# State-space groups: the second turn of xs moved into the middle of the gate chunk, its copy moved ahead of that gate

## The reference

```
def mamba2_bidir_mixer(x, w_in, conv_w, conv_b, dt_bias, a_log, d_skip, norm_w, w_out):
    zxbcdt = x @ w_in
    z, xbc, dt = jnp.split(zxbcdt, [SSM_D_INNER, SSM_D_INNER + SSM_CONV_DIM], axis=-1)
    xbc = jax.nn.silu(depthwise_conv_centred(xbc, conv_w, conv_b))
    xs, bm, cm = jnp.split(xbc, [...], axis=-1)
    dt = jax.nn.softplus((dt + dt_bias).astype(jnp.float32))
    y_f = ssd_chunked(xs, dt_f, a_neg[0], bm, cm)
    y_b = flip(ssd_chunked(flip(xs), flip(dt_b), a_neg[1], flip(bm), flip(cm)))
    y = (y_f + y_b).astype(x.dtype) + xs * d_skip[:, None]
    y = y.reshape(bsz, t, SSM_D_INNER) * jax.nn.silu(z)
    yg = yg * lax.rsqrt(jnp.mean(jnp.square(yg), -1, keepdims=True) + RMS_EPS)
    ...
    return y @ w_out
```

## Time and profile before

| | us |
|---|---|
| median of 3 runs | 1288.05 |
| lowest and highest | 1287.56, 1288.16 |
| the profiled execution's own time | 1287.21 |
| its span, first to last instruction | 1285.4 |
| TensorE busy in the span | 1254.6 |
| VectorE, ScalarE, GpSimd busy | 894.6, 711.4, 155.2 |
| mean granted TensorE clock | 0.995 of full |

### The profile page before, as it was taken

One profiled execution on the slowest core, in us unless ns is written; L12 is line 12 of the kernel. 1 busy time (PEld: TensorE's weight loads), 2 busy tenths in 40 slices (PEclk: granted clock), 3 DMA queues, 4 the chain that ended last, 5 costly groups with the idle time before them and its releaser, 6 DMA issues.

```text
span 1285.4 us, 19450 instructions
## 1 busy us (share of the span) xinstructions
PE 1254.6 (98%) x7940; PEld 1121.1 (87%) x7940; DVE 894.6 (70%) x1148; ACT 711.4 (55%) x909; POOL 155.2 (12%) x171
## 2 busy tenths in 40 slices
PE   8999999999799999999999999999999999999997
PEld 7889888889689888889888888889999989988886
DVE  6866656566866755568777665678899886866666
ACT  5445554455665555444764444447997873544442
POOL 0000000005604000010010000020325432100000
PEclk9999999999899999999999999999999999999999
DMA  8676665645059666666147555545544435555551
GB/s 281 201 227 178 209 196 179 200 152 191 34 147 213 204 191 196 197 164 215 66 135 255 199 185 184 187 144 161 157 153 122 153 99 193 201 196 196 196 190 41
DMA packets 214888, 224.52 MB, mean 175 GB/s; under 512 B 7312, under 2 KB 192016, under 8 KB 214672
## 3 DMA queue, kind: packets, MB, share of 16 engines
q1 hardware_dynamic: 211472, 213.41, 52.1%
q10 hardware_dynamic: 2304, 7.77, 1.8%
q0 software_dynamic: 1024, 2.10, 1.0%
HBM read 222.20 MB, written 1.05 MB: 174 GB/s over the span
## 4 chain that ended last, share of the span: by engine, by line
PE 84%; DVE 9%; ACT 3%; issue 2%; POOL 1%; DMA 1%; SPq 0%; DVEq 0%; ACTq 0%
PE ps L521 21%; PE ps L748 18%; PE ps L512 12%; PE ps L532 7%; PE ps L542 5%; PE ps L710 5%; PE ps L1040 3%; PE ps L504 3%; DVE wlo L1653 2%; PE ps L493 2%; PE ps L495 2%; PE ps L494 2%; DVE ssm_taps L2107 1%; ACT whi L1155 1%; PE ps L1021 1%
## 5 line engine op out<-in xcount | busy, mean ns | idle before, releaser
L1653 DVE TENSOR_TENSOR wlo<-raw,whi 128x2048 fp32r<-128x2048 f32 x199 | 456.5, 2300 | 127.0 <-ACT whi L1155 126.4
L1155 ACT ACTIVATE whi<-raw 128x2048 fp32r<-128x2048 f32 x202 | 385.3, 1910 | 87.9 <-PE ps L748 29.8
L521 PE MATMUL ps<-act,whi 128*128 128x512 f32 x1200 | 285.3, 390 | 0.4 <-DVE sum_sb L1796 0.4
L521 PEld LDWEIGHTS ps<-act,whi 128*128 128x128 f32 x1200 | 223.2, 188 | 45.7 <-DVE sum_sb L1796 0.7
L512 PEld LDWEIGHTS ps<-act,wlo 128*128 128x128 f32 x1416 | 180.8, 191 | 6.8 <-DVE wlo L1653 1.0
L512 PE MATMUL ps<-act,wlo 128*128 128x256 f32 x1416 | 183.9, 283 | 0.5 <-DVE wlo L1653 0.5
L1212 ACT ACTIVATE low_sb<-ps 128x512 f32<-128x512 f32 x88 | 52.4, 596 | 200.0 <-PE ps L512 199.9
L532 PE MATMUL ps<-whi,act 128*128 128x256 f32 x736 | 133.1, 285 | 1.1 <-DVE act L1734 1.1
L532 PEld LDWEIGHTS ps<-whi,act 128*128 128x128 f32 x736 | 113.5, 192 | 2.7 <-DVE act L1734 1.3
L1796 DVE TENSOR_TENSOR sum_sb<-ps,low_sb 128x512 f32<-128x512 f32 x88 | 60.5, 688 | 76.4 <-ACT low_sb L1212 76.3
L748 PE MATMUL ps<-whi,hidhi 128*128 128x512 f32 x336 | 104.2, 391 | 0.2 <-DVE sum_sb L1796 0.2
(11 more groups left out here) (238 smaller groups left out, 1848.4 us busy)
## 6 DMA issues: line engine op xcount, KB each, us to landing
raw<-in_mlp_w SPq DMA_DIRECT2D x128, 512.0 KB, 4.5
raw<-in_ffn_w_gate_up SPq DMA_DIRECT2D x88, 512.0 KB, 5.2
raw<-in_ssm_w_in SPq DMA_DIRECT2D x50, 512.0 KB, 4.8
raw<-in_ffn_w_down SPq DMA_DIRECT2D x44, 512.0 KB, 4.9
raw<-in_conv_w_in SPq DMA_DIRECT2D x24, 512.0 KB, 4.9
raw<-in_attn_w_in SPq DMA_DIRECT2D x18, 512.0 KB, 4.9
raw<-in_ssm_w_out SPq DMA_DIRECT2D x16, 512.0 KB, 4.5
raw<-in_attn_w_qkv SPq DMA_DIRECT2D x12, 512.0 KB, 4.4
```

Source lines behind the costliest of these rows:

```text
L521: e.matmul(bank2(b + f), hi[:, k, f * P:(f + 1) * P], act[:, :, k, :], start=k == 0, stop=False, skip_group_check=True)
L1155: e.activation(whi[s][:, :], raw[s][:, :], ACT.Copy).then_inc(*rounded.up(c))
L1653: e.tensor_tensor(wlo[s][:, :], raw[s][:, :], f32(whi[s][:, :]), ALU.subtract).then_inc(*split_by_vector.up(c))
```

## The change

On TensorE the turn of tile 1 of xs leaves its place behind step 5 (and, in groups 1 to 3, behind that step's outputs) and is issued inside step 5's chunk, between the 24 products of tile 0 and the 24 of tile 1. On ScalarE `copy_xs(G, 1)` moves from the head of the next group (in the last group, from behind the loop) to the place right ahead of `z_gate(2G + 1)`. Nothing is added or removed.

```diff
@@ pe_program, ssm @@
                         elif c is not None:
-                            token_chunk(c)
+                            token_chunk(c, None, [lambda: turn_xs(G, 1)] if k == 5 else ())
                             free[c % SLOTS] = z_gated(2 * G + k // 3)
...
                         if G == 0 and k == 5:
                             turn_parts()
-                        if k >= 4:
-                            turn_xs(G, k - 4)
+                        if k == 4:
+                            turn_xs(G, 0)
@@ act_program, ssm @@
                 for G in range(4):
                     n0 = 4 * (G - 1)
 
-                    if G:
-                        copy_xs(G - 1, 1)
                     if G == 1:
                         copy_gram(0)
...
                     conv_silu(4 * G + 3, G, 3)
+                    copy_xs(G, 1)
                     z_gate(2 * G + 1)
-                copy_xs(3, 1)
```

## The result

The changed kernel takes 1289.91 us (median of 20 runs, 1288.66 to 1293.95), the kernel before 1287.71 (20 runs beside it). The ratio is 1.0018, with a 95% interval of 1.0012 to 1.0024: 2.3 us slower, 1.5 to 3.1. The profiled execution has a span of 1288.0 us against 1285.4. Forecast were 1289.5 for the median, 1288.7 for the profiled execution, which took 1289.84, and a difference within 0.2%.

What follows compares the result with a forecast made beforehand. TensorE, busy 1254.6 of 1285.4 us, was taken as the bound. Group 0's 1.43 plus 0.10 for groups 1 to 3 gave 1.5 us, on 1288.05 a median of 1289.5; 8-in-10 range 1287.6 to 1290.9.

Steps and rivals of the forecast that it cites:

- Group 0: TensorE, chunk 5: the turn waits 0.96 us for ScalarE's bank read, plus 0.47 for transposes and refill; 1.43 later.
- It lasts: The 1.34 us wait ahead of item 1's outputs moves along with TensorE, so the 1.43 is carried through whole.
- rival 1: The delay is swallowed by the wait at 921.46; only about 0.2 us stays, 1288.2; chance 16%.
- Groups 1 to 3: TensorE: the moved turn doesn't wait; 0.05 us each in groups 1 and 2, 0 in group 3; 0.1 together.
- rival 2: The turn waits in all four groups, up to 0.96 us each, 1292.4; chance 11% with its lesser form.
- its lesser form: The same 1.4 us with a knock-on wait of about 1.3 in groups 0 and 1, 1290.8; within rival 2's 11%.
- ScalarE: Copy of xs and gate change places, 0.48 us apart, the next rounding keeping its time; worth 0.
- Rival 3: The copy ahead of the gate takes 0.48 us off each group's way to the next rounding, 1286.1; chance 4%.
- Group 3's wait for exponent rows shrinks by about 0.5: TensorE's 1.64 us wait in group 3 is shortened by the 0.47 added before it; no change in time.
- The clock: TensorE stays at full clock; a fall behind the moved turn, 8 us over four groups, 1297.5, had chance 2%.
- The rule weighed in the prediction: Transposes don't count as busy for the clock gate, which speaks against putting them with a wait into a chunk.
- the 1.5 of the mechanism: Sum over the groups, 1.43 in group 0 plus 0.10 in groups 1 to 3: 1.5 us slower; chance 67%.

Runs made afterwards that it cites:

- read_first: Changed kernel, but in group 0 ScalarE reads chunk 4's product out of its bank ahead of the rounding before it; ratio 1.0011 to the kernel before.
- before_again: The kernel before, unaltered, profiled once more; not timed against itself; its stretches sum to 196.59 us, as in the first profile.
- g0_only: Kernel before with the turn moved into the gate chunk in group 0 alone and the copy ahead of the gate in all groups; ratio 1.0012.
- g3_old: Kernel before with the turn moved in groups 0 to 2, left in its old place in group 3; ratio 1.0007.
- copy_first_old: Kernel before, but in group 0 ScalarE copies xs(0, 0) ahead of the exponent parts; ratio 0.9995.
- kept_busy: Changed kernel with seven unread 512-column matmuls in TensorE's wait for group 3's exponent rows, the gram-copy wait moved ahead of them; ratio 1.0006 to the kernel before.
- best_busy: Kernel best with six unread 512-column matmuls in front of the first product of y; median 1285.75 us, ratio 0.9985 to the kernel before.
- g3_only: Kernel before with the turn moved in group 3 alone and the copy ahead of the gate in all groups; ratio 1.0003.
- best: copy_first_old with, in group 3, VectorE making the exponent rows ahead of item 10's outputs; ratio 0.9990 to the kernel before.
- after_again: The changed kernel, unaltered, timed and profiled a second time; ratio 1.0013 to the kernel before.
- g0_old: Kernel before with the turn moved in groups 1 to 3 alone and the copy ahead of the gate in all groups; ratio 1.0004.
- copy_first_new: Changed kernel, but in group 0 ScalarE copies xs(0, 0) ahead of the exponent parts; ratio 1.0016 to the kernel before.

## Why the prediction was right, and where it was not

**Group 0.** The forecast was 0.96 of wait and 0.47 for transposes and refill, 1.43 in all. Measured were 1.45, and in read_first the two parts apart, 1.02 and 0.44. The grown wait (1.18, forecast about 1.2) shows that the old place gave nothing back. This is the one step that decides the sign.

**It lasts.** The wait in front of item 1 stayed (1.37), so rival 1 falls: "to item 1" is 22.98 or 22.99 in every kernel but the four that copy xs(0, 0) first.

**Groups 1 to 3.** The forecast was 0.1, measured was 0.06. There was no wait in front of the turn in any of them, so rival 2 falls with its lesser form.

**ScalarE.** The pair stands 0.47 apart in the other order in group 1, and the rounding behind it moved with TensorE (the first row is the kernel before's rounding, the others are the changed kernel's):

```profile
945.92 1.91 ACT L1155 ACTIVATE whi<-raw 128x2048 fp32r<-128x2048 f32 x1
...
945.95 0.57 ACT L1479 ACTIVATE xs<-ps 128x512 f32<-128x512 f32 x1
946.43 0.59 ACT L1401 ACTIVATE z<-ps 128x512 f32<-128x512 f32 x1
946.90 1.91 ACT L1155 ACTIVATE whi<-raw 128x2048 fp32r<-128x2048 f32 x1
```

The rounding starts 0.98 later by the span's time, which is the 1.45 less the 0.46 of the earlier start. Rival 3 falls.

**A sign that failed.** "Group 3's wait for exponent rows shrinks by about 0.5": it is 1.66 against 1.64. The 0.47 added ahead of the wait had been counted, the 0.36 to 0.44 taken away ahead of the same wait had not. It changed no sum.

**The clock.** This is the term that was missing. The prediction read the clock as 1.00 in the stretches that it had, took that as evidence that the mixture at the end of group 3 is safe, and gave a fall 2%, at a price of 8 us and in the wrong place, behind the turn in the chunk. The pace that it took for the lower level was right (0.205 a product, measured 0.21). The fall came at the end of group 3, in six of six profiles with the turn gone from there and the waits left as they were, and in none of the five with turn and waits as before (before, before_again, g0_only, g3_old, copy_first_old). It cost 1.0 to 2.4 us in them. Two interventions with matmuls in the idle time (kept_busy, best_busy) took it away, and this much of the cause is shown: the fall needs TensorE's idle time. That the missing transposes bring it is not shown. The profiles make it look like a rule. The timed executions say that it is at most a matter of how often, with 61% low against 41%. In g3_only, which has nothing but this difference and the swap of copy and gate, 8 of 11 are low against 12 of 27 of the kernel before beside it, too few to tell. So chance from one execution to the next stands as a rival that one profile of a kernel can't exclude.

The rule weighed in the prediction, of the Trainium skill ("TensorE: Matmul & The Clock Gate", Part 4, PE-mode transpose), says that transposes don't count as busy in the same way as other matmuls. By it, taking four away should leave the clock alone. The profiles of before and g3_only, whose other stretches are equal, speak against this, and the mean clocks of their timed executions, 0.9932 and 0.9934, don't. The runs settle it neither way.

**Why the number came out near.** Forecast were 1.5, measured 2.3 (1.5 to 3.1). The profiled execution has 1.45 + 0.06 + 1.12, and it took 1289.84, 1.1 more than the 1288.7 forecast for it. That the median of 1289.91 is only 0.4 over its forecast is in part luck: the forecast had added 0.84 for the distance between median and profiled execution, and in the changed kernel that distance was 0.07. How much of the median's rise is the fall is not settled. In g3_only it is 0.4 us in time against 2.3 in its profile. Among executions at 0.994 or above the changed kernel (14, both series) has a median of 1289.35 and the kernel before (61) one of 1287.58, 1.8 apart, nearer to the 1.5 of the mechanism. Open also is what decides between fall and full clock in an execution: the wait ahead of the decays is 1.64 in both before and g3_only, and what differs is the four transposes ahead of it.

## What to carry to other kernels

Before a step is moved forward on the engine that is the bound, find the instruction that releases it, and compare that one's end with the new place in each round of the loop, the first above all: here the other rounds had 2.4 us and more to spare by the forecast's rows and waited nowhere, and the first was 0.96 short. Whether the old place cost anything is the second question: work that stands in front of a wait for something else is free, and moving it into the stream makes it paid. And where the engine waits in a stretch of small matmuls, the granted clock is a quantity that an edit can tip: read it by stretches after the change, compare the mean clock over many executions of both kernels before a fall is put down to the edit, and try matmuls in the wait whose product nobody reads.

## What the runs showed of the hardware

The granted clock fell to 0.50 behind a single idle time of 1.64 to 1.66 us, in the turns of y or just behind them, and in best behind one of 1.36. In after_again, g0_old and g3_only the fall stands ahead of the second idle time, so that one did not bring it. The lower level lasted some 3 to 7 us, in which a product of 256 columns took 0.21 and not 0.12. The same idle times passed at full clock in five profiles. Three of the fourteen profiles (read_first, copy_first_new, best) also had a fall between 347 and 353, in code that no edit touches and where the kernel before shows none; here read_first's:

```profile
349.00:352.00 3.00, 3.00 (x20) 2.34 (x21) 2.86 (x13) 1.65 (x3) 2.75 (x4) 0.50 0.00 0
```

So at some places the fall is chance from one execution to the next, and the count above says the same of the end of group 3. Matmuls whose product nobody reads held the level in both cases tried. They cost nothing that the table shows, since they ran where TensorE would have stood.
